# Gated delta rule, gating unit: prompt values turned in 32x32 squares on VectorE instead of on TensorE

## The chip, the cores and the metric

The kernel runs on one core of one Trainium2 chip, in one launch. The metric is the device time of that launch in microseconds (us). The core has a matrix engine (TensorE, PE in the rows; its weight loads PEld), a vector engine (VectorE, DVE), a scalar engine (ScalarE, ACT), GpSimd (POOL), which here mostly issues transfers, and SyncE (SP), which issues the weight loads from HBM. Each engine runs its own instructions in program order and waits for others on semaphores.

## The reference

Two layers of a decoder trunk, for a prompt of 1024 tokens and 8 samples of 4 tokens. Layer 0 has gated delta rule heads (mixer A) and chunked spatial gating groups (mixer B); layer 1 has mLSTM heads; each layer has a squared-ReLU MLP of width 4096. What the change touches is mixer B of layer 0:

```
def spatial_gating(u, v, w_s, b_s):          # chunks of C = 128 tokens, 4 groups of 128 channels
    w = jnp.where(causal_mask(C), w_s[:, :C, :C], 0.0)
    vc = v.reshape(B, NC, C, G_B, DG_B)
    z = jnp.einsum('gpq,bnqgc->bnpgc', w, vc) + b_s[:, :C].T[None, None, :, :, None]
    return u * z.reshape(u.shape).astype(u.dtype)
...
proj = h @ w_in
qkv, gate, beta_pre, a_pre, u_pre, v_pre = split_cols(proj, ...)
u = jax.nn.gelu(u_pre)
vb = rmsnorm(jax.nn.gelu(v_pre).reshape(B, L, G_B, DG_B), sgu_norm_g)
o_b = spatial_gating(u, vb, sgu_w, sgu_b)
```

The product over `q` contracts tokens, so the values `vb` must stand with tokens on the partitions, while the projection leaves them with channels on the partitions. Something must turn each tile of 128 tokens by 4 groups of 128 channels.

## The kernel before

**The dense work.** Every large product of the trunk (`piece`) is done three times over on split operands (high times high, low times high, high times low), and fills TensorE nearly without a gap. It goes in units of 24 steps; each unit needs its own 512 KB of weights, which SyncE loads, ScalarE splits into a high part (`whi`, function `hi`) and VectorE into a low part (`wlo`, function `lo`, line L1788). TensorE may begin a unit only when `wlo` of it is there (`w_split`). `whi` is made of the next unit only when TensorE has begun the present one, and stands in ScalarE's queue behind whatever the program put ahead of it. At the end of a unit ScalarE copies the result out of PSUM.

**The mixer.** Between pieces of dense work stand the steps of the delta rule, in an order that `Plan` writes out once for all engines (`gdn`): for a tile of 128 tokens `act`, `sum`, `dec`, `kk`, `kT`, `vT`, then `b1` to `b4` (the inverse of the triangular matrix, its 16x16 blocks by VectorE in `b1` to `b3`), `la` and `lb` for each level, `vn`, `zw`, `o`, `oT`. Tiles 0 to 3 lie beside the input projection of layer 0, tiles 4 to 7 beside the output projection and the first MLP; a ninth tile (`TILES`) holds the 32 sample tokens and has steps of its own (`gdn_rows`).

**Step `dec` before.** TensorE turns the four groups of values with four transposes (L899) into PSUM (`M4(3)`), and signals `vsT`. ScalarE takes the exponential `E`, waits for `vsT`, squares the four groups out of PSUM, takes the logarithm, then waits for `du` (VectorE's `Dm`, L2129) and takes its exponential `D`, then `dtu` (L2133) and its exponential `DTe`, and last copies the four groups, scaled, into `VB` (`vsr`). These ten or so instructions stand ahead of ScalarE's next unit end and next `whi`. VectorE's step `kk` begins with `A` (L2140), which needs `D`; `A` goes through HBM twice (`base_blocks` on GpSimd: out and in ahead of `b1`, out and in ahead of `b4`), and VectorE's `b4` (L2174) lets TensorE's first `la` go. TensorE's `vT` needs `vsr` (the bank `M4(3)`) and `ke` (L2145, which needs `DTe`).

**The loads.** GpSimd issues a tile's operands in `gdn_x` (L2703): chunks 0 to 11 (query, key, value of mixer A), chunks 20 to 23 (values of the gating unit) with channels on the partitions, each one transfer.

Of the kernel before, what the change touches and what calls it, by code (L numbers as in the profile page):

```python
# [8 lines left out]
ACT = mybir.ActivationFunctionType  # L9

P = 128
D = 1024
# [3 lines left out]
NS = NB * LS  # L16
T = NP + NS
TILES = NP // P
H = 4
# [309 lines left out]
def build(nc, x_prompt, x_sample, state_gdn, state_gdn_conv, state_mlstm_c, state_mlstm_n, state_mlstm_m,  # L329
# [4 lines left out]
    with ctx:  # L334
# [293 lines left out]
        def _(pe):  # L628
# [244 lines left out]
            def gdn(t, step, q):  # L873
# [9 lines left out]
                if step == "sum":  # L883
# [5 lines left out]
                        w("vns", t)  # L889
                    s(mm(M4(0)[:, :, 0:n], ones[:, :], m["SQ"][:, 4:8, :]), "ss")  # L890
                    s(mm(M4(1)[:, :, 0:n], ones[:, :], m["SQ"][:, 0:4, :]), "ss")
                elif step == "dec":
                    if t:
                        w("on", t)
                        w("ofa", t)
                    if g:
                        w("act", t - 3)
                    for h in range(H):
                        last = pe.transpose(M4(3)[0:n, h, :], X[:, 20 + h, :], ident[:, :])  # L899
                    s(last, "vsT")  # L900
                elif step == "kk":
                    w("kn")
                    for h in range(H):
# [4 lines left out]
                        last = mm(M4(1)[0:n, h, 0:n], QH[:, 4 + h, :], QH[:, h, :])  # L908
                    s(last, "kq")
                elif step == "kT":  # L910
                    for h in range(H):
                        last = pe.transpose(M4(2)[0:n, h, :], QH[:, 4 + h, :], ident[:, :])
                    s(last, "kT")
                elif step == "vT":
                    w("vsr")
                    w("ke")
                    w("state")
                    for h in range(H):
                        pe.matmul(M4(3)[:, h, :], X[:, 8 + h, :], ident[:, :], is_transpose=True,
                                  start=True, stop=False)  # L920
                        last = mm(M4(3)[:, h, :], m["KB"][:, h, :], St[:, h, :], start=False, stop=True)
# [46 lines left out]
                        s(last, "x")  # L968
                elif step == "zw":
                    w("inv", inv_at(t, lv - 1, 1))  # L970
                    for h in range(H):
                        last = mm(M4(0)[:, h, 0:n], m["VB"][0:n, h, :], WT[0:n, h, 0:n])
                    s(last, "z")
                elif step == "vn":
                    w("inv", inv_at(t, lv - 1, 1))
                    for h in range(H):
                        last = mm(M4(1)[:, h, :], m["XiT"](h), m["RU"][:, h, :])
                    s(last, "vnew")
                elif step == "o":
                    w("vns")  # L980
                    w("qd")
                    for h in range(H):
                        mm(M4(2)[:, h, :], m["QD"][:, h, :], St[:, h, :], start=True, stop=False)
                        last = mm(M4(2)[:, h, :], m["DT"][:, h, :], m["VN"][:, h, :], start=False, stop=True)
                    s(last, "o")
                    for h in range(H):
                        last = mm(M4(3)[:, h, :], m["KD"][:, h, :], m["VN"][:, h, :])
                    s(last, "ds")
                elif step == "oT":
                    w("on")  # L990
                    w("state", t + 2)
                    for h in range(H):
                        last = pe.transpose(M4(3)[:, h, 0:n], m["ON"][0:n, h, :], ident[0:n, 0:n])
                    s(last, "oT")
# [263 lines left out]
        def _(act):  # L1258
# [257 lines left out]
            def gdn(t, step, q):  # L1516
# [3 lines left out]
                w = lambda name, v=t + 1: act.wait_ge(S("g_" + name), v)  # L1520
                s = lambda ins, name: ins.then_inc(S("g_" + name), 1)
                if step == "act":
                    w("xin", 32 * (t + 1))
                    if t:
                        w("qd", t)
                        w("inv", inv_at(t - 1, LB, 0))
# [12 lines left out]
                elif step == "dec":  # L1539
                    w("bc", 16 * (t + 1))  # L1540
                    s(A_(m["E"], m["KB"], ACT.Exp), "E")
                    w("vsT")
                    for h in range(H):
                        last = A_(m["VB"][0:n, h, :], M4(3)[0:n, h, :], ACT.Square, accum_out=small[0:n, 0, h:h + 1])
                    after(mine(last))
                    vssl = mine(A_(small[0:n, 1, :], small[0:n, 0, :], ACT.Ln, bias=epsc[0:n, :], scale=1.0 / P))
                    w("du")
                    s(A_(m["Dm"], m["Dm"], ACT.Exp, scale=-1.0), "D")
                    after(vssl)
                    vssr = mine(A_(small[0:n, 2, :], small[0:n, 1, :], ACT.Exp, scale=-0.5))  # L1550
                    w("dtu")
                    s(A_(m["DT"], m["DT"], ACT.Exp), "DTe")
                    after(vssr)
                    for h in range(H):
                        last = A_(m["VB"][0:n, h, :], M4(3)[0:n, h, :], ACT.Copy, scale=small[0:n, 2, h:h + 1])
                    s(last, "vsr")
                elif step == "vT" and n == NS:
                    w("vT")
# [208 lines left out]
        def _(dve):  # L1767
# [341 lines left out]
            def gdn(t, step, q):  # L2109
# [15 lines left out]
                elif step == "dec":  # L2125
# [6 lines left out]
                    for h in range(H):  # L2132
                        last = STT(m["DT"][0:n, h], m["KB"][0:n, h], gc[:, h:h + 1], mn[:, :],  # L2133
                                   ALU.subtract, ALU.add)
                    s(last, "dtu")
                elif step == "kk":
                    w("D")
                    w("kk")
# [387 lines left out]
        def _(pool):  # L2526
# [173 lines left out]
            def gdn_x(t, late):  # L2700
# [22 lines left out]
                if t:  # L2723
                    pool.wait_ge(S("g_qn"), t)
                    pool.wait_ge(S("g_vT"), t)
                if t == TILES:
                    pool.wait_ge(S("g_lo"), t)
                load(0, 12, "g_xin")
                load(20, NCH, "g_xin")
                if t not in (0, 4):  # L2730
                    decay_rows(t)
                if t == TILES:
# [231 lines left out]
```

## Time and profile before

| | |
|---|---|
| median of 3 runs | 2590.41 us (2590.01 to 2590.78) |
| profiled execution | 2587.41 us |
| its span in the trace | 2585.0 us |
| mean granted TensorE clock over the span | 0.992 |
| TensorE, VectorE, ScalarE, GpSimd busy | 97%, 53%, 43%, 10% of the span |

The profile is of one execution. The span runs from the first to the last instruction in the trace; 2.4 us of the execution lie around it. The profiled execution is 3.0 us shorter than the median of the runs. In the rows "L630" is the one line through which all matmuls go; which product it is shows in the names (`dense` or `mixer`). L1267 is ScalarE's one line in the same way. `arena` is the mixer's working memory.

### The profile page before, as it was taken

The numbers are of one execution on the slowest core, as the hardware profiler recorded it, in microseconds if no ns is written. First come the engines' busy times: TensorE is split into PE (matmuls) and PEld (weight loads), VectorE is DVE, ScalarE is ACT, GpSimd is POOL, SyncE is SP. The second block draws the span as 40 slices with busy tenths as digits, with TensorE's granted clock in tenths as the row PEclk, the third lists the DMA queues.
The fourth block names the chain that finished last, engine by engine and source line by source line (L and its number), as shares of the span: only waits on it lengthen the run. The fifth ranks groups of instructions, "written<-read, shape, count | busy, mean of one in ns | idle before, by whom it ended". The sixth has DMA issues, their size and how long they took to land.

```text
span 2585.0 us, 40052 instructions
## 1 busy us (share of the span) xinstructions
PE 2519.1 (97%) x16699; PEld 2255.0 (87%) x16699; DVE 1362.7 (53%) x2215; ACT 1114.0 (43%) x1869; POOL 261.1 (10%) x421
## 2 busy tenths in 40 slices
PE   8998989999999999999999999999999999999999
PEld 7778888787787798899999989998887988999998
DVE  4746764655565565434444465535554466443344
ACT  6554446454555344333333345434333345323324
POOL 4121111100001001100001001111111000000000
PEclk9999999999999999999999999999999999999999
DMA  6563335533334366544333235554445343333222
GB/s 206 160 165 109 107 108 138 161 91 96 110 91 118 91 175 186 156 120 114 107 90 106 91 116 171 166 146 134 122 133 157 115 143 98 98 107 115 83 89 84
DMA packets 369396, 321.52 MB, mean 124 GB/s; under 512 B 12601, under 2 KB 340339, under 8 KB 369216
## 3 DMA queue, kind: packets, MB, share of 16 engines
q1 hardware_dynamic: 336224, 207.91, 27.6%
q0 software_dynamic: 32992, 111.06, 14.5%
q8 instruction: 132, 2.16, 0.4%
q14 instruction: 48, 0.39, 0.0%
HBM read 261.33 MB, written 57.58 MB: 123 GB/s over the span
## 4 chain that ended last, share of the span: by engine, by line
PE 85%; DVE 6%; ACT 5%; DMA 2%; issue 2%; POOL 0%; DVEq 0%; ACTq 0%; POOLq 0%
PE dense L630 77%; PE mixer L630 6%; DVE wlo L1788 1%; ACT arena L1267 1%; ACT whi L1267 1%; DVE arena L2022 1%; DVE arena L2024 0%; DVE hf L1929 0%; ACT relu L1267 0%; DMA arena<-xrow 0%; PE mixer L696 0%; ACT L1267 0%; ACT L1272 0%; DVE arena L2258 0%; ACT h1hi L1267 0%
## 5 line engine op out<-in xcount | busy, mean ns | idle before, releaser
L630 PE MATMUL dense<-hhi,whi 128*128 128x272 f32 (+1 forms) x3072 | 847.4, 330 | 22.1 <-DVE wlo L1788 16.9
L630 PE MATMUL dense<-hhi,wlo 128*128 128x272 f32 (+1 forms) x3072 | 826.9, 324 | 0.0
L630 PE MATMUL dense<-hlo,whi 128*128 128x272 f32 (+1 forms) x3072 | 825.7, 323 | 0.0
L1788 DVE TENSOR_TENSOR wlo<-wst,whi 128x1024 fp32r<-128x1024 f32 x384 | 469.4, 1222 | 230.3 <-ACT whi L1267 229.4
L630 PEld LDWEIGHTS dense<-hhi,whi 128*128 128x128 f32 x3072 | 517.2, 189 | 77.3 <-DVE wlo L1788 22.4
L1267 ACT ACTIVATE whi<-wst 128x1024 fp32r<-128x1024 f32 x384 | 403.7, 1051 | 416.5 <-PE dense L630 409.4
L630 PEld LDWEIGHTS dense<-hhi,wlo 128*128 128x128 f32 x3072 | 515.5, 190 | 41.7
L630 PEld LDWEIGHTS dense<-hlo,whi 128*128 128x128 f32 x3072 | 517.8, 190 | 38.2 <-issue 0.7
L630 PE MATMUL dense<-h1hi,whi 128*128 128x272 f32 (+1 forms) x1536 | 422.3, 329 | 11.9 <-DVE wlo L1788 5.8
L630 PE MATMUL dense<-h1hi,wlo 128*128 128x272 f32 (+1 forms) x1536 | 413.5, 323 | 0.0
L630 PE MATMUL dense<-h1lo,whi 128*128 128x272 f32 (+1 forms) x1536 | 411.6, 322 | 0.0
L630 PEld LDWEIGHTS dense<-h1hi,whi 128*128 128x128 f32 x1536 | 256.6, 188 | 41.0 <-DVE wlo L1788 10.0
L1804 DVE TENSOR_TENSOR h1lo<-relu,h1hi 128x544 fp32r<-128x544 f32 (+1 forms) x128 | 90.5, 707 | 358.8 <-ACT relu L1267 358.6
L630 PEld LDWEIGHTS dense<-h1hi,wlo 128*128 128x128 f32 x1536 | 256.8, 188 | 21.4
L630 PEld LDWEIGHTS dense<-h1lo,whi 128*128 128x128 f32 x1536 | 256.6, 188 | 20.7 <-issue 0.5
L1267 ACT ACTIVATE relu<-dense 128x512 f32<-128x512 f32 (+2 forms) x132 | 80.4, 609 | 352.1 <-PE dense L630 352.1
L630 PEld LDWEIGHTS mixer<-arena 128*128 128x128 f32 (+4 forms) x2012 | 142.5, 149 | 42.8 <-issue 20.8
L630 PE MATMUL mixer<-arena 128*128 128x128 f32 (+8 forms) x2012 | 165.6, 257 | 14.4 <-DVE arena L2174 6.4
L1863 DVE TENSOR_TENSOR accA<-dense,accA 128x512 f32<-128x512 f32 (+1 forms) x168 | 116.7, 699 | 91.1 <-PE dense L630 90.5
L1879 DVE TENSOR_TENSOR ssum<-ssum,sq 128x512 f32<-128x512 f32 (+1 forms) x98 | 69.2, 706 | 125.8 <-ACT sq L1267 125.7
L1267 ACT ACTIVATE ffh<-dense 128x512 f32<-128x512 f32 (+5 forms) x124 | 62.2, 525 | 167.0 <-PE dense L630 154.9
L2642 POOL DMA_DIRECT2D proj<-ffh x96 | 52.6, 549 | 462.6 <-ACT ffh L1267 374.6
(398 smaller groups left out, 1792.4 us busy)
## 6 DMA issues: line engine op xcount, KB each, us to landing
wst<-in_w_ff_dram SPq DMA_DIRECT2D x256, 512.0 KB, 3.9
wst<-in_w_in_even_dram SPq DMA_DIRECT2D x48, 512.0 KB, 4.1
wst<-in_w_in_odd_dram SPq DMA_DIRECT2D x48, 512.0 KB, 3.9
proj<-ffh POOLq DMA_DIRECT2D x48, 272.0 KB, 2.6
proj<-ffh POOLq DMA_DIRECT2D x48, 256.0 KB, 2.3
arena<-proj POOLq DMA_DIRECT2D x24, 512.0 KB, 4.9
out_dram<-arena POOLq DMA_DIRECT2D x17, 512.0 KB, 4.7
wst<-in_w_out_even_dram SPq DMA_DIRECT2D x16, 512.0 KB, 4.0
```

Source lines behind the costliest of these rows:

```text
L630: return pe.matmul(out, lhsT, rhs, start=start, stop=stop)
L1267: return act.activation(out, in_, func, **how)
L1788: TT(wlo[:, u % 2, :], wst[:, u % 2, :], whi[:, u % 2, :].bitcast(F32), ALU.subtract)\
L1804: TT(h1lo[:, k, 0:n], r, h1hi[:, k, 0:n].bitcast(F32), ALU.subtract)\
L1863: TT(v, out_of(key, g), v, ALU.add).then_inc(S("dve_evac"), 1)
L1879: ins = TT(ssum[:, 0:n], ssum[:, 0:n], sq2[:, c % 2, 0:n], ALU.add)
L2022: link(TT(tmp, left.unsqueeze(2).broadcast_to([NBLK, b, b, b]), right.rearrange("p j c -> p c j").unsqueeze(1).broadcast_to([NBLK, b, b, b ...
L2642: dma(proj[l][c, :, G0[g]:G0[g] + n], pout2[:, i % 2, 0:n]).then_inc(S(f"stored{i % 2}"), 16)
```

## The change

- **TensorE.** The four transposes of step `dec` go for tiles 0 to 7. Waits that stood there move: `on` to step `kT`, `ofa` to `vT`; `vT` no longer waits for `vsr`, which `zw` now does.
- **GpSimd.** For tiles 0 to 7 the load of chunks 20 to 23 becomes four transfers of 32 partitions each, which put 32x32 squares at the places where they must stand after a full turn. Only the inside of each square is then still unturned.
- **VectorE.** One transpose of 128x512 in 32x32 squares, after `dtu` in step `dec` and ahead of `A` (and of a `wlo`, where the plan has one between them).
- **ScalarE.** `D` now comes before the wait for `vsT`, and `DTe` before the small exponential. Squares and scaled copies read from the working memory instead of PSUM, for prompt tiles.

```
@@ TensorE @@
-                elif step == "dec":
-                    if t:
-                        w("on", t)
-                        w("ofa", t)
-                    if g:
-                        w("act", t - 3)
-                    for h in range(H):
-                        last = pe.transpose(M4(3)[0:n, h, :], X[:, 20 + h, :], ident[:, :])
-                    s(last, "vsT")
@@
                 elif step == "kT":
+                    if t:
+                        w("on", t)
@@
                 elif step == "vT":
-                    w("vsr")
                     w("ke")
                     w("state")
+                    if t:
+                        w("ofa", t)
@@
                 elif step == "zw":
                     w("inv", inv_at(t, lv - 1, 1))
+                    w("vsr")
@@ ScalarE @@
                 if step == "act":
-                    w("xin", 32 * (t + 1))
+                    w("xin", 80 * t + (32 if n == NS else 80))
@@
                 elif step == "dec":
                     w("bc", 16 * (t + 1))
                     s(A_(m["E"], m["KB"], ACT.Exp), "E")
+                    w("du")
+                    s(A_(m["Dm"], m["Dm"], ACT.Exp, scale=-1.0), "D")
                     w("vsT")
-                    for h in range(H):
-                        last = A_(m["VB"][0:n, h, :], M4(3)[0:n, h, :], ACT.Square, accum_out=small[0:n, 0, h:h + 1])
+                    if 0 < t < TILES:
+                        w("ds", t)
+                    values = m["VB"] if n == P else M4(3)[0:n]
+                    for h in range(H):
+                        last = A_(m["KD" if n == P else "VB"][0:n, h, :], values[:, h, :], ACT.Square,
+                                  accum_out=small[0:n, 0, h:h + 1])
                     after(mine(last))
                     vssl = mine(A_(small[0:n, 1, :], small[0:n, 0, :], ACT.Ln, bias=epsc[0:n, :], scale=1.0 / P))
-                    w("du")
-                    s(A_(m["Dm"], m["Dm"], ACT.Exp, scale=-1.0), "D")
+                    w("dtu")
+                    s(A_(m["DT"], m["DT"], ACT.Exp), "DTe")
                     after(vssl)
                     vssr = mine(A_(small[0:n, 2, :], small[0:n, 1, :], ACT.Exp, scale=-0.5))
-                    w("dtu")
-                    s(A_(m["DT"], m["DT"], ACT.Exp), "DTe")
                     after(vssr)
                     for h in range(H):
-                        last = A_(m["VB"][0:n, h, :], M4(3)[0:n, h, :], ACT.Copy, scale=small[0:n, 2, h:h + 1])
+                        last = A_(m["VB"][0:n, h, :], values[:, h, :], ACT.Copy, scale=small[0:n, 2, h:h + 1])
                     s(last, "vsr")
@@ VectorE, end of step dec @@
+                    if g:
+                        w("act", t - 3)
+                    else:
+                        w("xin", 80 * (t + 1))
+                    if t:
+                        w("oT", t)
+                    s(dve.transpose(rows_of(m["VB"]), rows_of(X[:, 20:NCH])), "vsT")
@@ GpSimd, gdn_x @@
+                    pool.wait_ge(S("g_vsT"), t)
...
                 load(0, 12, "g_xin")
-                load(20, NCH, "g_xin")
+                if t == TILES:
+                    load(20, NCH, "g_xin")
+                else:
+                    squares = X[:, 20:NCH].rearrange("p c (b i) -> p (c b) i", i=32)
+                    for a in range(4):
+                        c0 = t * P + 32 * a
+                        dma(squares[32 * a:32 * a + 32],
+                            proj[0][20:NCH, :, c0:c0 + 32].rearrange("c (b j) i -> j (c b) i", j=32))\
+                            .then_inc(S("g_xin"), 16)
```

**ScalarE in tile 4**, from the exponential `E` (which waits for `g_bc`) to the next `whi`. Here `arena<-mixer` is a read out of PSUM, and `accA<-dense` and `sq<-accA` belong to the output projection. Before:

```order
L1267 ACTIVATE arena<-arena 128x512 [waits g_bc]
L1267 ACTIVATE arena,small<-mixer 128x128 [waits g_vsT]
L1267 ACTIVATE arena,small<-mixer 128x128 x3
L1267 ACTIVATE small<-small,epsc 128x4 [waits act_step]
L1267 ACTIVATE arena<-arena 128x512 [waits g_du]
L1267 ACTIVATE small<-small 128x4 [waits act_step]
L1267 ACTIVATE arena<-arena 128x512 [waits g_dtu]
L1267 ACTIVATE arena<-mixer,small 128x128 [waits act_step]
L1267 ACTIVATE arena<-mixer,small 128x128 x3
L1267 ACTIVATE accA<-dense 128x512 [waits job_done]
L1267 ACTIVATE sq<-accA 128x512 [waits act_evac,squares_added]
L1267 ACTIVATE whi<-wst 128x1024 [waits w_loaded1,w_used]
```

And now:

```order
L1262 ACTIVATE arena<-arena 128x512 [waits g_bc]
L1262 ACTIVATE arena<-arena 128x512 [waits g_du]
L1262 ACTIVATE arena,small<-arena 128x128 [waits g_ds,g_vsT]
L1262 ACTIVATE arena,small<-arena 128x128 x3
L1262 ACTIVATE small<-small,epsc 128x4 [waits act_step]
L1262 ACTIVATE arena<-arena 128x512 [waits g_dtu]
L1262 ACTIVATE small<-small 128x4 [waits act_step]
L1262 ACTIVATE arena<-arena,small 128x128 [waits act_step]
L1262 ACTIVATE arena<-arena,small 128x128 x3
L1262 ACTIVATE accA<-dense 128x512 [waits job_done]
L1262 ACTIVATE sq<-accA 128x512 [waits act_evac,squares_added]
L1262 ACTIVATE whi<-wst 128x1024 [waits w_loaded1,w_used]
```

The exponential that waits for `g_du` has moved ahead of the squares, which wait for `g_vsT`, now VectorE's signal.

**VectorE in tile 2**, from `Dm` to `ke` (`ffh` is the convolution beside it). Before:

```order
L2129 SCALAR_TENSOR_TENSOR arena<-arena,cols,maskpos 128x128 [waits g_bc,dve_step]
L2129 SCALAR_TENSOR_TENSOR arena<-arena,cols,maskpos 128x128 x3
L2133 SCALAR_TENSOR_TENSOR arena<-arena,cols,masknegT 128x128 x4
L1788 TENSOR_TENSOR wlo<-wst,whi 128x1024 [waits w_hi]
L1827 SCALAR_TENSOR_TENSOR ffh<-ffh,par 128x512 [waits act_evac]
L1830 SCALAR_TENSOR_TENSOR ffh<-ffh,par 128x32
L2140 SCALAR_TENSOR_TENSOR arena<-mixer,cols,arena 128x128 [waits g_kk,g_D,dve_step]
```

And now:

```order
L2128 SCALAR_TENSOR_TENSOR arena<-arena,cols,maskpos 128x128 [waits g_bc,dve_step]
L2128 SCALAR_TENSOR_TENSOR arena<-arena,cols,maskpos 128x128 x3
L2132 SCALAR_TENSOR_TENSOR arena<-arena,cols,masknegT 128x128 x4
L2141 STREAM_TRANSPOSE arena<-arena 128x512 [waits g_oT,g_xin]
L1787 TENSOR_TENSOR wlo<-wst,whi 128x1024 [waits w_hi]
L1826 SCALAR_TENSOR_TENSOR ffh<-ffh,par 128x512 [waits act_evac]
L1829 SCALAR_TENSOR_TENSOR ffh<-ffh,par 128x32
L2146 SCALAR_TENSOR_TENSOR arena<-mixer,cols,arena 128x128 [waits g_kk,g_D,dve_step]
```

One instruction is inserted, ahead of a `wlo` and of `A`; the others keep their order.

## Rows read from the trace of the kernel before

The line numbers are those of the kernel before.

**Rows 1.** Page, part 1: busy us (share of the span) xinstructions.
```profile
PE 2519.1 (97%) x16699; PEld 2255.0 (87%) x16699; DVE 1362.7 (53%) x2215; ACT 1114.0 (43%) x1869; POOL 261.1 (10%) x421
```

**Rows 2.** Timeline, TensorE, tile 5: start us, us, engine, line, operation [idle before].
```profile
568.17 0.60 PE L899 MATMUL mixer<-ident,arena 128*128 128x128 f32 x4
568.52 0.48 PE L630 MATMUL dense<-h1hi,whi 128*128 128x512 f32 x1
568.84 0.39 PE L630 MATMUL dense<-h1lo,whi 128*128 128x512 f32 x1
569.06 0.40 PE L630 MATMUL dense<-h1hi,wlo 128*128 128x512 f32 x1
```

**Rows 3.** Line L2185, VectorE: duration ns min/median/max.
```profile
L2185 DVE STREAM_TRANSPOSE arena<-arena x8: 310/311/313, 178.1 to 785.4; 128x128 f32<-128x128 f32 x8
```

**Rows 4.** Timeline, VectorE and GpSimd, mLSTM tile 0.
```profile
1167.53 1.42 DVE L2362 STREAM_TRANSPOSE arena<-arena 128x256 f32<-128x256 f32 x4
...
1170.47 3.13 POOL L2839 DMA_DIRECT2D arena<-proj  x4
```

**Rows 5.** Timeline, ScalarE, VectorE and TensorE, tile 4.
```profile
425.18 0.25 ACT L1267 ACTIVATE arena<-mixer 128x128 f32<-128x128 f32 x1
...
426.33 0.30 ACT L1267 ACTIVATE small<-small,epsc 128x4 f32<-128x4 f32 x1
...
428.14 0.63 ACT L1267 ACTIVATE arena<-arena 128x512 f32<-128x512 f32 x1 [0.33 <-DVE arena L2133]
...
428.68 1.12 ACT L1267 ACTIVATE arena<-mixer,small 128x128 f32<-128x128 f32 x4
...
429.68 0.61 ACT L1267 ACTIVATE accA<-dense 128x512 f32<-128x512 f32 x1
...
426.98 1.13 DVE L2133 SCALAR_TENSOR_TENSOR arena<-arena,cols,masknegT 128x128 f32<-128x128 f32 x4
...
434.49 1.21 DVE L1788 TENSOR_TENSOR wlo<-wst,whi 128x1024 fp32r<-128x1024 f32 x1
...
435.76 0.52 PE L630 MATMUL dense<-hhi,whi 128*128 128x272 f32 x2 [1.00 <-DVE wlo L1788]
```

**Rows 6.** Timeline, VectorE and TensorE, tile 6.
```profile
663.16 1.23 DVE L1788 TENSOR_TENSOR wlo<-wst,whi 128x1024 fp32r<-128x1024 f32 x1 [0.25 <-ACT whi L1267]
...
665.42 0.40 PE L630 MATMUL dense<-h1hi,whi 128*128 128x512 f32 x1
```

**Rows 7.** Timeline, VectorE and TensorE, tile 7.
```profile
748.39 1.23 DVE L1788 TENSOR_TENSOR wlo<-wst,whi 128x1024 fp32r<-128x1024 f32 x1 [2.67 <-ACT whi L1267]
...
750.95 0.39 PE L630 MATMUL dense<-hhi,whi 128*128 128x512 f32 x1
```

**Rows 8.** Timeline, VectorE and TensorE, tiles 1 to 3.
```profile
210.81 1.12 DVE L2140 SCALAR_TENSOR_TENSOR arena<-mixer,cols,arena 128x128 f32<-128x128 f32 x4
...
237.05 0.62 PE L630 MATMUL mixer<-arena 32*32 32x16 f32 x32 [5.38 <-DVE arena L2174]
...
345.79 0.82 PE L630 MATMUL dense<-hhi,whi 128*128 128x272 f32 x2 [6.34 <-DVE wlo L1788]
```

**Rows 9.** TensorE's timeline, then windows: us, busy of PE, PEld, DVE, ACT, POOL, PEclk, DMA share, GB/s.
```profile
600.30 0.71 PE L630 MATMUL dense<-hhi,whi 128*128 128x512 f32 x1 [1.93 <-DVE wlo L1788]
...
600.00:604.00 4.00, 3.70 (x9) 2.94 (x10) 2.17 (x3) 1.45 (x2) 0.92 (x1) 0.57 0.63 164
```

**Rows 10.** Timeline, ScalarE, VectorE and TensorE, sample tile.
```profile
830.15 0.25 ACT L1267 ACTIVATE arena<-mixer 32x128 f32<-32x128 f32 x1
...
830.96 0.35 DVE L2063 SCALAR_TENSOR_TENSOR arena<-arena,gcol,maskposS 128x128 f32<-128x128 f32 x1
...
835.65 0.50 PE L630 MATMUL dense<-h1hi,whi 128*128 128x512 f32 x1 [0.51 <-DVE h1lo L1804]
```

**Rows 11.** Timeline, TensorE, tile 0.
```profile
155.44 0.30 PE L919 MATMUL mixer<-ident,arena 128*128 128x128 f32 x1 [1.06 <-ACT arena L1267]
...
170.31 0.50 PE L630 MATMUL dense<-hhi,whi 128*128 128x512 f32 x1 [1.40 <-DVE wlo L1788]
```

## The prediction

> **What bounds the kernel now.** I read the page first. TensorE is busy 97% of the span and no other engine is near [rows 1], so the end is set by TensorE's instructions plus its waits. Each change has to be read as one or the other. Next I went through the timeline of TensorE around each of the eight tiles, looking for gaps and for who ended them. Last I read ScalarE and VectorE just ahead of those gaps. What a reader is to see there: most of TensorE's waits near the mixer end with a `wlo` or with `b4`, both VectorE's, and behind `wlo` stands a `whi` of ScalarE. So the question is not only what TensorE saves but what ScalarE and VectorE now do later.
>
> **What TensorE saves.** In tile 5 the four transposes begin at 568.17 and the next dense product at 568.52, which is 0.35 us; that product is followed after 0.32 us, where the next pair stands 0.22 us apart [rows 2]. So a group costs about 0.35 + 0.09 = 0.44 us, and eight groups 3.5 us. The mean duration of such a transpose is no help, since they overlap. The saving counts only where TensorE does not wait for somebody else soon after.
>
> **What VectorE pays.** The trace has no 128x512 transpose in squares. A 128x128 one took 0.311 us [rows 3]; four of 128x256 took 1.42 us together, 0.355 us each [rows 4]. From above the price is two of the latter, 0.71 us, from below one of them, 0.36 us. Between them I go by pace: a `wlo` of 1024 columns took 1.21 us [rows 5], so half as many columns are worth 0.61 us, which I take.
>
> **What GpSimd pays.** The mLSTM loads its values in the same way; issuing four such transfers took 3.13 us [rows 4]. They replace one issue, so GpSimd is at most 3.1 us later per tile. Behind them stand the row of decays for the next tile and the stores of the projection; the values themselves are wanted half a tile later. I cost this at nothing. The cover is that distance of tens of us; without it 3.1 us a tile would show.
>
> **What ScalarE pays.** This is the step that I think decides. Before, the squares began when TensorE's transposes were done (425.18 in tile 4), while VectorE was still at `Dm`. ScalarE then had only `D`, the small exponential, `DTe` and the copies left: VectorE's `dtu` ended at 426.98 + 1.13 = 428.11, `DTe` began at 428.14, the copies at 428.68, and ScalarE was free at 429.68 [rows 5]. Now the squares wait for VectorE's transpose, which ends at about 428.11 + 0.6 = 428.7. Behind it come the squares, 426.33 - 425.18 = 1.15 us, the logarithm, 0.30, `DTe`, 428.68 - 428.14 = 0.54, and the small exponential, some 0.1 [rows 5]. The copies begin at 430.8 instead of 428.68: **ScalarE is 2.1 us later** wherever VectorE was the one waited for. The squares and copies now read from SBUF. The nearest rows are an exponential of 128x512 from SBUF, 0.63 us, and a copy of 128x512 from PSUM, 0.61 us [rows 5], so 0.02 us each or 0.2 us over eight, which I leave out of the sum; it is inside the range.
>
> The Trainium skill ("VectorE: DVE Perf Modes", section "The TRN2 errata — SBUF-src ops pay a fixed extra latency per instruction") gives ScalarE 224 fixed cycles from SBUF and 172 from PSUM at 1.2 GHz. That is an estimate of 0.35 us for the eight instructions, which in tiles 4, 6 and 7 would add 1.0 us to the sum below. The rows above show less of it, and the sum goes by them.
>
> **Tile by tile.**
> *Tile 0:* nothing. TensorE waited 1.06 us for `vsr`, and this wait goes. But it also waits at 170.31 for a `wlo` [rows 11]; ahead of that `wlo` ScalarE and VectorE work on without a gap on instructions whose total is unchanged, and TensorE's start there stays where it was.
> *Tiles 1 to 3:* `A` follows `dtu` directly in tile 1, at 210.81, and from there the way through HBM and `b1` to `b3` leads to TensorE's wait of 5.38 us at 237.05; in tile 3 a `wlo` behind `b3` ends a wait of 6.34 us [rows 8]. Tile 2 is built alike. Here VectorE's chain sets the time, not TensorE: its 0.61 us more delay each tile by 0.6 us, TensorE's saving is swallowed, and so is ScalarE's 2.1 us, which is less than the waits. Together **+1.8 us**.
> *Tile 4:* TensorE waits 1.00 us for the `wlo` that begins at 434.49 [rows 5]. VectorE gets there by way of a sum of squares for which ScalarE's copies must be done, then `A`, `ke` and two more without a gap. The 2.1 us go straight through: TensorE starts at 437.9 instead of 435.76, **+2.1 us**, and its wait grows to some 3.5 us.
> *The clock:* after a wait of 1.93 us the granted clock was 0.57 over the next four us, with products at 0.63 us where they take 0.40 [rows 9, 2]; this is mostly the lower of TensorE's two levels, 1.2 instead of 2.4 GHz. The loss is 0.43 x 3.70 = 1.6 us. I expect it behind tile 4's long wait. Part of it falls on TensorE while it would wait for the norm's chain, so I take **+1.4 us**.
> *Tile 5:* no unit begins there while ScalarE is late: **-0.4 us**.
> *Tile 6:* from the start of a `wlo` to TensorE's first product were 435.76 - 434.49 = 1.27 us [rows 5]. `wlo` at 663.16 allowed 664.43, TensorE needed it at 665.42: a slack of 1.0 us [rows 6]. Late by 2.1, it costs **+1.1 us**.
> *Tile 7:* 748.39 + 1.27 = 749.66 against 750.95, a slack of 1.3 us [rows 7]: **+0.8 us**.
> *Sample tile:* its squares began at 830.15, ahead of `Dm`; now they follow `D`, which needs VectorE's `Dm`, done at 830.96 + 0.35 = 831.31. That is some 1.3 us later for the copies and all behind them, and TensorE already waits for an `h1lo` at 835.65 [rows 10]: **+1.3 us**.
>
> The sum is 0 + 1.8 + 2.1 + 1.4 - 0.4 + 1.1 + 0.8 + 1.3 = 8.1 us. On the profiled execution's 2587.4 us this gives 2595.5 us. The median of the runs shown was 3.0 us above that execution, so I forecast 2590.4 + 8.1 = 2598.5, rounded to **2598 us**. The likeliest case's own range is 2594 to 2602: the transpose between 0.36 and 0.71 us moves seven tiles by -0.25 to +0.1 us each, and the clock's loss may be none.
>
> **The rivals.**
> *Faster.* ScalarE's lateness never reaches a `wlo` that TensorE wants, because ScalarE catches up in its idle time, and VectorE's `D` comes sooner. For it speaks that ScalarE is idle more than half the span [rows 1] and that tile 0 loses a wait of 1.06 us [rows 11]. Then TensorE keeps its 3.5 us, perhaps the 1.06 too: 2586 to 2587 us. Against it stands the slack of only 1.0 and 1.3 us in tiles 6 and 7. It decides if ScalarE is late by less than 1.0 us. Chance 0.12.
> *Half covered, no clear change.* Tiles 6, 7 and the sample tile hide it, and the clock stays up: 1.8 + 2.1 - 3 x 0.4 = +2.7, so 2593 us. Chance 0.25.
> *The clock falls more often.* Each new wait, in tiles 2, 6 and 7, brings the low level. Three times 1.6 us on top: 2603 us. For it speaks the wait of 1.93 us, after which the first product took 0.71 us [rows 9]; against it that of 1.00 us, after which the first took 0.52 [rows 5]. Chance 0.08.
> *The squares in HBM.* The transfers in pieces of 32 numbers hold up a weight load or a store. Were each tile late by the 3.13 us of issuing alone [rows 4], the eight would cost 25 us, 2615. The mLSTM does it without TensorE waiting for it, so 0.05. The Trainium skill ("DMA: Bandwidth & Descriptors", section "Why small descriptors are slow (HBM only)") speaks for this case: each descriptor carries fixed costs that weigh most below 256 bytes. No row here shows what that does to this load.
> The forecast has the remaining 0.50.
>
> **How the numbers follow.** A measurement of this kernel can tell about 0.2% from no change, 5.2 us. Slower than 2595.6 are most of the forecast (0.43 of 0.50), the clock and the transfers: 0.57 with a little of the second rival. Within the bound lie the rest of the forecast and nearly all of the second rival: 0.31. Faster is 0.12. The range runs from 2588, which takes in the second rival and the edge of the first, to 2603.
>
> **What the profile of the changed kernel would show.** Right: in tile 4, ScalarE's copies at about 2.1 us further behind `Dm` than before and a wait of TensorE for `wlo` of 3 us or more, with the granted clock below 1 behind it; new waits for `wlo` of 1 us or so in tiles 6 and 7; the waits for `b4` in tiles 1 to 3 still there; the transpose at 0.6 to 0.7 us. Wrong: TensorE without new waits from tile 4 on, `DTe` or the copies at their old distance from `Dm`, or the squares' transfers landing so late that ScalarE's `act` waits for them.

## The result, and the profile after

Before 2590.21 us (median of 6 runs, 2585.59 to 2590.94), after 2600.32 us (6 runs, 2595.82 to 2603.27). The ratio is 1.0044, 95% interval [1.0034, 1.0054]: slower by 10 us by the medians and by some 11 by the ratio. A second set of five runs of the same changed kernel gave 2599.53 us against 2587.51 us, 1.0052 [1.0038, 1.0066].

The profiled execution of after took 2603.27 us, the slowest of its six, with a span of 2601.5 us. Page, part 1, to lay beside [rows 1]:

```profile
PE 2522.2 (97%) x16667; PEld 2255.6 (87%) x16667; DVE 1368.3 (53%) x2223; ACT 1117.0 (43%) x1869; POOL 275.7 (11%) x445
```

TensorE has 32 instructions fewer and its busy time is no shorter; VectorE has gained 5.6 us, ScalarE 3.0, GpSimd 14.6. The busy shares explain nothing. The waits of TensorE do (us in total, times, longest us):

```profile
PE dense L630 <- DVE wlo L1787: 27.4, 18, 4.7
PE mixer L630 <- DVE arena L2180: 7.0, 2, 5.1
PE mixer L913 <- DVE arena L2151: 5.9, 4, 2.1
...
PE dense L630 <- DVE h1lo L1803: 3.6, 4, 1.9
```

Before, `wlo` had stood at 22.6 us in 15 waits, `b4` (now L2180) at 6.4, `h1lo` (the low part of the MLP's activations) at 1.9. The third line is new: TensorE's `vT` (L913) waits for VectorE's `ke` (L2151).

To place the loss I took the start of the same TensorE instruction in both traces and followed the difference. It was 0.2 us at 140, 3.8 behind tile 0, 4.3 behind tile 3 (425), 8.6 behind tile 4 (481), 8.1 at 568, 12.2 behind the sample tile (836), 16.7 at 1985. A single trace of before is a poor zero, though, and so is one of after. That is what the second pair of profiles below is for.

**Tile 4**, the timeline of after for ScalarE, VectorE and TensorE, then a window behind the wait (us, busy of PE, PEld, DVE, ACT, POOL, PEclk, DMA share, GB/s):

```profile
433.51 0.31 ACT L1262 ACTIVATE arena<-arena 128x128 f32<-128x128 f32 x1 [1.04 <-DVE arena L2141]
...
434.83 0.30 ACT L1262 ACTIVATE small<-small,epsc 128x4 f32<-128x4 f32 x1
435.03 0.62 ACT L1262 ACTIVATE arena<-arena 128x512 f32<-128x512 f32 x1
...
435.77 1.28 ACT L1262 ACTIVATE arena<-arena,small 128x128 f32<-128x128 f32 x4
436.96 0.57 ACT L1262 ACTIVATE accA<-dense 128x512 f32<-128x512 f32 x1
...
432.77 0.70 DVE L2141 STREAM_TRANSPOSE arena<-arena 128x512 f32<-128x512 f32 x1
438.29 0.69 DVE L1878 TENSOR_TENSOR ssum<-ssum,sq 128x512 f32<-128x512 f32 x1 [4.81 <-ACT sq L1262]
438.90 1.12 DVE L2146 SCALAR_TENSOR_TENSOR arena<-mixer,cols,arena 128x128 f32<-128x128 f32 x4
...
441.73 1.22 DVE L1787 TENSOR_TENSOR wlo<-wst,whi 128x1024 fp32r<-128x1024 f32 x1
...
443.00 0.52 PE L630 MATMUL dense<-hhi,whi 128*128 128x272 f32 x2 [3.99 <-DVE wlo L1787]
...
444.00:448.00 4.00, 4.00 (x17) 2.96 (x16) 1.23 (x1) 2.84 (x4) 2.72 (x6) 0.57 0.93 286
```

This is the chain of the prediction. `Dm` began at 425.93 before and begins at 430.67 here. From there the copies stand at +5.10 us instead of +2.75, so ScalarE is 2.35 us later. `wlo` stands at +11.06 instead of 434.49 - 425.93 = +8.56, later by 2.50. TensorE's wait is 3.99 us instead of 1.00, and the granted clock behind it is 0.57, most of the time at the lower level, where the kernel before had 1.00. The squares go from 433.51 to the logarithm at 434.83, 1.32 us where [rows 5] had 1.15; the copies free ScalarE after 1.19 us instead of 1.00.

**Tiles 6 and 7 and the sample tile**, TensorE's timeline of after; in [rows 6, 7] the first two had no wait, in [rows 10] the third had 0.51:

```profile
673.46 0.50 PE L630 MATMUL dense<-h1hi,whi 128*128 128x512 f32 x1 [1.82 <-DVE wlo L1787]
...
761.66 0.51 PE L630 MATMUL dense<-hhi,whi 128*128 128x512 f32 x1 [1.51 <-DVE wlo L1787]
...
847.84 0.50 PE L630 MATMUL dense<-h1hi,whi 128*128 128x512 f32 x1 [1.85 <-DVE h1lo L1803]
```

**Tiles 1 to 3**, which I had not foreseen in this form. VectorE in tile 3, then TensorE in tiles 1 to 3, then the window behind the first of these waits:

```profile
330.83 0.70 DVE L2141 STREAM_TRANSPOSE arena<-arena 128x512 f32<-128x512 f32 x1
331.45 1.08 DVE L2146 SCALAR_TENSOR_TENSOR arena<-mixer,cols,arena 128x128 f32<-128x128 f32 x4
333.73 0.69 DVE L2151 SCALAR_TENSOR_TENSOR arena<-arena 128x512 f32<-128x512 f32 x1 [1.19 <-ACT arena L1262]
...
218.28 0.33 PE L913 MATMUL mixer<-ident,arena 128*128 128x128 f32 x1 [1.96 <-DVE arena L2151]
...
276.82 0.41 PE L913 MATMUL mixer<-ident,arena 128*128 128x128 f32 x1 [2.11 <-DVE arena L2151]
...
334.48 0.33 PE L913 MATMUL mixer<-ident,arena 128*128 128x128 f32 x1 [1.17 <-DVE arena L2151]
...
219.00:223.00 4.00, 4.00 (x23) 4.00 (x21) 2.25 (x8) 2.90 (x9) 2.55 (x4) 0.59 0.20 29
```

The diff put `DTe` behind the squares. So in tiles 1 and 3 VectorE, done with `A`, waits 1.19 us for `DTe` ahead of `ke`, and TensorE's `vT` waits for `ke`, though it lost its wait for `vsr`. In tile 2 it is not `DTe`: a `wlo` and the convolution stand between the transpose and `A` there, `ke` follows `A` without a gap, and TensorE waits 2.11 us all the same.

**The parts' prices.** VectorE's transpose (duration ns min/median/max, first and last start us), and the loads in squares on GpSimd with their time to landing:

```profile
L2141 DVE STREAM_TRANSPOSE arena<-arena x8: 702/703/708, 151.4 to 755.1; 128x512 f32<-128x512 f32 x8
...
L2742 POOL DMA_DIRECT2D arena<-proj x32: 649/653/675, 132.5 to 680.5; - x32
...
DMA to landing us min/median/max: 4.7/6.1/7.2
```

### The profile page after: what moved, and what is told of

Read it like the earlier page. It is cut to its first block, busy times and chain, and to the rows that moved or that the text cites. A ratio compares the mean times of both kernels' runs of the same rounds, so it can differ in the third digit from the quotient of the medians.

```text
span 2601.5 us, 40036 instructions
## 1 busy us (share of the span) xinstructions
PE 2522.2 (97%) x16667; PEld 2255.6 (87%) x16667; DVE 1368.3 (53%) x2223; ACT 1117.0 (43%) x1869; POOL 275.7 (11%) x445
## 4 chain that ended last, share of the span: by engine, by line
PE 77%; DVE 5%; ACT 4%; issue 2%; DMA 1%; POOL 0%; DVEq 0%; ACTq 0%; POOLq 0%
PE dense L630 71%; PE mixer L630 5%; DVE wlo L1787 1%; ACT arena L1262 1%; ACT whi L1262 1%; ACT relu L1262 0%; DVE hf L1928 0%; ACT h1hi L1262 0%; DVE arena L2264 0%; DVE hlo L1924 0%; PE mixer L1181 0%; DVE accA L1862 0%; DVE arena L2021 0%; DMA arena<-in_state_mlstm_c_dram 0%; DMA out_dram<-arena 0%
```

## The experiments

The twelve experiments came in three groups of four. The kernel before ran beside each group, with medians of 2586.28, 2587.51 and 2587.14 us, and each ratio below is to the kernel before of its own group. The expectations of the first group were written in us from the 2590 of the first measurement, so compare the ratios. Theory A: ScalarE's lateness, by way of `wlo` and `ke`, is the loss. Its rival B: the loads in squares and GpSimd's longer work are.

**DTe ahead of the squares.**

```diff
 s(A_(m["Dm"], ..., ACT.Exp, scale=-1.0), "D")
+w("dtu")
+s(A_(m["DT"], m["DT"], ACT.Exp), "DTe")
 w("vsT")
...
-w("dtu")
-s(A_(m["DT"], m["DT"], ACT.Exp), "DTe")
```

> The change, with one step of ScalarE moved: the exponential of DT (DTe) stands ahead of the four squares instead of behind them. Theory A (order on ScalarE): in the changed kernel VectorE waits 1.19 us ahead of ke for DTe in each prompt tile, and TensorE's vT then waits 1.2 to 2.1 us for ke in tiles 1 to 3. Both waits go; the copies stay as late as they were, so the waits for wlo in tiles 4, 6 and 7 stay in part. Time 3 to 6 us below the changed kernel's 2600.3, so 2594 to 2597. Theory B (the loads in pieces and the longer work of GpSimd cost the time, from tile 0 on): no clear difference from the changed kernel, 2599 to 2601.

Measured: 2599.43 us, 1.0051 [1.0038, 1.0064]. No gain. VectorE's gap ahead of `ke` went (`ke` follows `A` after 1.00 us in tiles 1 and 3) and the waits at `vT` fell from 5.9 us in 4 to 2.8 in 2; that of tile 2 stayed at 2.10. What TensorE did not wait for at `vT` it waited for later: in tile 1 the wait at `vT` went from 1.96 to 0.67 us and that for `b4` from 5.14 to 6.83, in tile 3 the 1.17 us went and a wait for `wlo` grew from 0.66 to 1.56. The copies came at +4.72 us behind `Dm`, 0.4 earlier, and tile 4 still cost 4.8 us. So the wait at `vT`, the most striking new line of the profile, was not where the time went.

**The transpose early, ScalarE's old order.**

```diff
 elif step == "dec":
+    ... s(dve.transpose(rows_of(m["VB"]), rows_of(X[:, 20:NCH])), "vsT")
     w("bc", 16 * (t + 1))
     (Dm, DT)
-    ... s(dve.transpose(...), "vsT")
 ScalarE: E, squares, logarithm, D, small exponential, DTe, copies, as in the kernel before
```

> The change, with VectorE's transpose put ahead of Dm (and of its wait for bc) and ScalarE's steps in the order of the kernel before (E, squares, logarithm, D, small exponential, DTe, copies); the sample tile's order is thereby also the old one. Theory A: ScalarE is as early as before, D some 0.7 us later; vT's waits go, wlo in tiles 4, 6 and 7 is at its old place, h1lo in the sample tile waits 0.5 us again. TensorE keeps a part of its 3.5 us: 2587 to 2591. Theory B: tile 0 still costs 3.8 us and the whole stays at 2597 to 2600. A third (VectorE's 0.7 us in front of A is what costs): 2 to 4 us above the kernel before, 2592 to 2594.

Measured: 2594.52 us, 1.0027 [1.0018, 1.0037]. It lies between the expectations of A and B, and 7 us above its kernel before where the third had 2 to 4: about half of the loss came back. The copies are at +2.76 us behind `Dm` again in tiles 1 to 7. In its trace TensorE lost 1.0 us in tile 4 and nothing in tiles 6, 7 and in the sample tile's step at `h1lo`. Most of what stayed arose earlier: TensorE was 6.2 us behind the kernel before at 425. So in tiles 0 to 3 the loss did not go with ScalarE's lateness.

**One plain load.**

```diff
-squares = ...; for a in range(4): dma(squares[32 * a:32 * a + 32], ...)
+load(20, NCH, "g_xin")
```

> The change, but the values come with the one plain load of the kernel before instead of four loads of turned squares, so that the squares are turned within themselves but not in place: the delta rule's values are permuted, all instructions of the engines stay. It prices the loads and GpSimd's issues alone. Theory B: tile 0's 3.8 us go and the time falls by 4 to 10 us, to 2590 to 2596. Theory A: at most 1 us of the 3.8 goes, 2599 to 2601.

Measured: 2599.23 us, 1.0049 [1.0036, 1.0061]. Its trace had TensorE at -0.65 us behind tile 3 where after had +4.3, but the time is that of the changed kernel: against B as the main cause. (The second trace of after, below, stood at +0.4 there with the loads in squares, so the 4.3 was scatter in the main.)

**ScalarE's new order in the kernel before.**

```diff
+w("du"); s(A_(m["Dm"], ..., scale=-1.0), "D")
 w("vsT")
 (squares, logarithm)
-w("du"); s(A_(m["Dm"], ..., scale=-1.0), "D")
-(small exponential)
 w("dtu"); s(A_(m["DT"], m["DT"], ACT.Exp), "DTe")
+(small exponential)
```

> The kernel before (TensorE transposes, one load, no transpose on VectorE), with only ScalarE's steps in the order of the changed kernel: E, D, squares, logarithm, DTe, small exponential, copies. Theory A: the squares now begin behind D, some 1.5 us later than before, DTe behind them; half or more of the loss shows: 2594 to 2598, with waits of VectorE ahead of ke and of TensorE at vT. If instead VectorE's transpose or the loads cost the time: 2590 to 2592.

Measured: 2589.08 us, 1.0013 [1.0004, 1.0022], a quarter of the loss and less than A expected. ScalarE is late by 1.06 us here (copies at +3.81), not by 2.35. Tile 4's wait is twice what it was, and the sample tile's is that of the changed kernel; TensorE's timeline:

```profile
434.05 0.52 PE L630 MATMUL dense<-hhi,whi 128*128 128x272 f32 x2 [2.08 <-DVE wlo L1788]
...
835.37 0.50 PE L630 MATMUL dense<-h1hi,whi 128*128 128x512 f32 x1 [1.87 <-DVE h1lo L1804]
```

TensorE's difference grew by 0.8 us over tile 4 and by 1.35 in the sample tile. So ScalarE's order alone gives the sample tile's cost. In tile 4 the order alone makes less than half of the lateness (1.06 of 2.35 us); the rest is the transpose behind `dtu`, for which the squares wait, and 0.17 us by which the four squares are slower from SBUF.

**The two kernels again.**

> The changed kernel once more, unaltered, for a second profile and five more times beside the others. If the costs read in its first profile belong to the change, TensorE's offset against the kernel before is again some 3.8 us behind tile 0, 4.3 more from tile 4, 1.6 in tile 6, 1.8 in tile 7, 1.3 in the sample tile. What comes out otherwise is scatter from one execution to the next. The first profiled execution was the slowest of six, so the span should be 2 to 5 us shorter here; ratio to before 1.0035 to 1.0055.

> The kernel before once more, unaltered: it shows how far two profiles of one kernel differ. Expected: the same starts of TensorE within 1 us up to 1970 us; and at 1981 us, where the first profile had no fall of the clock behind the wait for the mLSTM's state and all others had one that cost 1.6 to 2 us, a coin's toss. Ratio 0.999 to 1.001.

Measured: after 2599.53 us, 1.0052 [1.0038, 1.0066]; before 2587.95 us, 1.0004 [0.9996, 1.0013]. TensorE's difference against the first trace of before, for both traces of after and the second of before, in us:

| stretch of before | after | after again | before again |
|---|---|---|---|
| tile 0, 140 to 188 | +3.6 | +2.1 | +0.1 |
| tiles 1 to 3, to 425 | +0.4 | -2.0 | -1.2 |
| tile 4, to 481 | +4.3 | +4.3 | -0.3 |
| tile 5's group, to 568 | -0.5 | -0.4 | 0 |
| 568 to 604 | -1.6 | -1.6 | -1.6 |
| tile 6, to 665.5 | +1.6 | +1.6 | 0 |
| 665.5 to 725 | +1.4 | -1.4 | +1.4 |
| tile 7, 725 to 751.5 | +1.3 | +1.3 | 0 |
| 751.5 to 830 | 0 | +1.3 | 0 |
| step at `h1lo`, 830 to 840 | +1.3 | +2.0 | 0 |
| 840 to 1975 | +2.2 | +1.2 | +0.5 |
| 1975 to 1985 | +2.3 | +3.6 | +0.3 |

What repeats to 0.1 us belongs to the change: tiles 4, 6 and 7. Tiles 1 to 3 scatter by more than 2 us. The row 568 to 604 is the fall of the clock in the first trace of before, which the second does not have though the wait ahead of it is the same. The row 665.5 to 725 is of the same kind: every trace has a wait of 2.68 us at the place where before has it (709.8), and the clock behind it differed from one execution to the next. Behind 840 comes nothing that the diff touches; the 4.1 and 5.1 us that the two traces of after lose from there to the end, where before again has 0.6, no experiment explains. TensorE's timeline and a window, of before again:

```profile
599.11 0.50 PE L630 MATMUL dense<-hhi,whi 128*128 128x512 f32 x1 [1.93 <-DVE wlo L1788]
...
598.00:602.00 4.00, 2.89 (x12) 2.36 (x13) 2.97 (x3) 2.23 (x3) 1.17 (x2) 1.00 0.52 156
```

**The loads in squares in the kernel before.**

```diff
-load(20, NCH, "g_xin")
+for a in range(4): dma(squares[32 * a:32 * a + 32], ...)   # tiles 0 to 7
```

> The kernel before, with only the load changed: the values come in four loads of turned squares, TensorE transposes them as before, so the delta rule's values are permuted. It prices GpSimd's issues and the transfers alone. Theory B (the loads cost some 1.2 us in each of tiles 0 to 2, as the offsets 4.3 against -0.65 of the changed kernel with and without them suggest): 3 to 5 us, 2589 to 2592 where before is 2586.3. Theory A (ScalarE's order and no more; the medians of the two, 1.0044 and 1.0049, say so): 0 to 1 us.

Measured: 2589.47 us, 1.0010 [1.0001, 1.0018], some 2.6 us, at the edge of what can be told. Its trace is of the slowest of its eleven runs; it lost 4.5 us in tile 0 and 0.6 from tile 4 on. Tile 0, TensorE at `b4`, first in the kernel before, which had the clock at 1.00 there, then here with the windows behind:

```profile
175.38 0.44 PE L630 MATMUL mixer<-arena 32*32 32x16 f32 x32 [0.70 <-DVE arena L2174]
...
178.46 0.44 PE L630 MATMUL mixer<-arena 32*32 32x16 f32 x32 [2.14 <-DVE arena L2174]
...
178.00:181.00 3.00, 2.54 (x38) 1.72 (x38) 0.69 (x3) 0.00 (x0) 0.00 (x0) 0.75 0.71 182
181.00:184.00 3.00, 3.00 (x41) 2.41 (x41) 1.48 (x4) 2.07 (x3) 0.56 (x1) 0.68 0.22 86
```

A first part of tile 0's loss stands further ahead, at ScalarE's `whi` near 142. It waits for a load of weights that SyncE issued near 132.3, beside the tile's own loads. ScalarE in the kernel before and here:

```profile
140.76 1.05 ACT L1267 ACTIVATE whi<-wst 128x1024 fp32r<-128x1024 f32 x1
...
142.12 1.06 ACT L1267 ACTIVATE whi<-wst 128x1024 fp32r<-128x1024 f32 x1 [1.20 <-DMA wst<-in_w_in_even_dram]
```

That load landed 9.8 to 10.0 us after its issue in five of the six traces with the loads in squares in tile 0, and 9.0 in the other (the first of after). In the eight with the plain load it took 8.0 to 8.3 us in five and 8.9 to 9.1 in three. ScalarE's wait was 1.2 to 1.4 us in the five, none to 0.5 in all others.

**D first in tiles 1 to 3 of the kernel before.**

```diff
+if t in (1, 2, 3): w("du"); s(A_(m["Dm"], ...), "D")
 w("vsT")
 (squares, logarithm)
-w("du"); s(A_(m["Dm"], ...), "D")
+if t not in (1, 2, 3): w("du"); s(A_(m["Dm"], ...), "D")
```

> The kernel before, with only D (the exponential of Dm) put ahead of the squares on ScalarE in tiles 1 to 3. A new theory C: ScalarE comes 1 us later to whi, frees the staging buffer of the weights later, and SP's next load of 512 KB then starts behind the small transfer of the diagonal blocks (arow) instead of ahead of it; that transfer landed 2.3 to 2.5 us after its issue in all kernels with D first and 3.8 to 4.3 us in those with the squares first. By C tiles 1 to 3 gain 2 to 4 us and nothing is lost behind them: 2582 to 2584. By the simpler view that a later ScalarE only costs: 2586 to 2588.

Measured: 2587.15 us, 0.9997 [0.9989, 1.0006]: no difference. In its trace VectorE's `b1` did come 1.7 us sooner behind `Dm` in tile 1, and TensorE at 425 stood at -1.4 us; but before again stood at -0.9 there with nothing changed. (`b1` waits for the diagonal blocks of `A` to come back from HBM.) Theory C is not shown by the times.

**The change in halves.** The whole change in some tiles only, the others as before.

```diff
+BY_DVE = (0, 1, 2, 3)      # second kernel: (4, 5, 6, 7)
 PE, ACT, DVE, POOL: the new path if t in BY_DVE, else the old one
```

> The change in tiles 0 to 3 alone (loads in squares, VectorE's transpose behind dtu, ScalarE's new order); tiles 4 to 7 and the sample tile are those of the kernel before. Theory A' (ScalarE's lateness costs where TensorE stands close behind it, which is from tile 4 on): the two profiles of the changed kernel had TensorE 0.4 and 4.3 us late behind tile 3, so 0 to 4 us: 2588 to 2592. Theory B' (a part of the loss that the profiles do not show cleanly sits in tiles 0 to 3): 2593 or more.

> The change in tiles 4 to 7 alone; tiles 0 to 3 and the sample tile are those of the kernel before. Theory A': both profiles of the changed kernel lost 4.3 us in tile 4, 1.6 in tile 6 and 1.8 in tile 7 and won 0.45 in tile 5: 7.3 us, so 2593 to 2596. Theory B': less than half of the loss, 2589 to 2591.

Measured: tiles 0 to 3 alone 2591.28 us, 1.0017 [1.0008, 1.0027]; tiles 4 to 7 alone 2593.36 us, 1.0023 [1.0012, 1.0034]. Together 1.0040, and with the sample tile's 1.3 us 1.0045: within their intervals of 0.1% each, the parts add up to the change's 1.0044 and 1.0052. In the second kernel tiles 4, 5, 6 and 7 cost +4.3, -0.5, +1.6 and +1.3 us, as in the table; TensorE in tiles 4 and 6:

```profile
438.64 0.59 PE L635 MATMUL dense<-hhi,whi 128*128 128x272 f32 x2 [3.99 <-DVE wlo L1814]
...
669.05 0.50 PE L635 MATMUL dense<-h1hi,whi 128*128 128x512 f32 x1 [1.82 <-DVE wlo L1814]
```

The first kernel's trace, of the slowest of its ten runs (2596.1 us), lost 4.5 us in tile 0 and 0.9 in tiles 1 to 3. GpSimd's read of `xrow`, the second round trip of the diagonal blocks through HBM, was issued at 174.39, and VectorE's `b4` began when it landed:

```profile
178.34 0.48 DVE L2208 TENSOR_SCALAR arena<-arena,halves 128x128 f32<-128x128 f32 x2 [3.01 <-DMA arena<-xrow]
...
178.88 0.44 PE L635 MATMUL mixer<-arena 32*32 32x16 f32 x32 [2.08 <-DVE arena L2208]
```

**The transpose early, in tiles 4 to 7 only.** The second experiment's place and order, once by itself and once with D first in tiles 1 to 3.

```diff
+BY_DVE = (4, 5, 6, 7)      # transpose ahead of Dm, squares ahead of D
+D_FIRST = ()               # last kernel: (1, 2, 3)
```

> VectorE turns the values in tiles 4 to 7 alone, with the transpose ahead of Dm and ScalarE's old order (as in the second experiment); all else is the kernel before. The profile of the second experiment had +1.0 us in tile 4, -0.45 in tile 5, -0.1 in tile 6 and 0 in tile 7. Theory A': no clear difference, 2586 to 2589. If VectorE's transpose or the load in squares costs something by itself in a stage where TensorE is the bound: 2590 or more.

> As the one with the early transpose in tiles 4 to 7, and D ahead of the squares on ScalarE in tiles 1 to 3 besides. It is the version that the parts found so far would make the fastest. By the sum of the parts (0.5 and -0.8 us): 2585 to 2588, not clearly below the kernel before; by theory C in full (2 to 4 us won in tiles 1 to 3): 2583 to 2585.

Measured: 2585.93 us, 0.9998 [0.9989, 1.0007], and 2586.22 us, 0.9994 [0.9985, 1.0003]. Moved ahead, VectorE's transpose costs nothing in tiles 4 to 7, and the waits in tiles 6 and 7 are gone. Against the experiment with the whole change in tiles 4 to 7, the loads in squares, the transposes and the missing work of TensorE are the same; only the places on VectorE and ScalarE differ, and the loss of 1.0023 is gone. But it gains nothing either. In tile 4 it stands in front of `Dm` and passes its 0.65 us on, TensorE's wait there being 2.26 us:

```profile
435.24 0.52 PE L635 MATMUL dense<-hhi,whi 128*128 128x272 f32 x2 [2.26 <-DVE wlo L1814]
```

That is +1.0 us in tile 4 against -0.5, -0.1 and -0.4 in the other three. (In the last kernel's trace tile 4 cost 2.4 us, since the clock fell behind the same wait.) The same place and order in all tiles had 1.0027, so the early transpose with its loads costs some 0.3%, 7 us, in tiles 0 to 3, and the late one, at 1.0017, not more (each ratio is good to 0.1%). No version was clearly faster than the kernel before.

## Why the prediction was right, and where its steps were off

The forecast of 2598 us in 2588 to 2603 met 2600.32, and the mechanism given the most weight holds: ScalarE's lateness, by way of `wlo`, from tile 4 on. Undoing it in tiles 4 to 7 takes 1.0023 to 0.9998. That the number came so close is in part luck. The loss forecast was 8.1 us; measured it was 10 by the medians, and 12 in the second set, where the kernel before stood at 2587.51 and not at the 2590.4 of the forecast. Two places stood at nothing in the sum and cost 2 to 4 us (tile 0) and 4 to 5 us (behind 840) in the traces, against less than the 1.8 us forecast in tiles 1 to 3; what else makes the sum fall only 2 to 4 us short is scatter of that size between executions. Step by step:

- *TensorE saves 0.44 us a tile.* In tile 5, the one that hides nothing, every trace with the transposes gone gained 0.44 to 0.48 us. Right.
- *VectorE pays 0.61 us.* The transpose took 0.70 us, and VectorE's next instruction began 0.63 us after its start. So 0.63 is what `A` is later by, and 0.70 what the squares wait for. The upper bound was misread: the 1.42 us of [rows 4] are four instructions that overlap, one of 128x256 took 0.40 us (median of 32), not 0.355.
- *ScalarE is 2.1 us later; reading from SBUF is left out.* The copies came 2.35 us later and ScalarE was free 2.5 us later. The some 0.4 us missing are VectorE's transpose, 0.09, and the reading from SBUF, 0.36: 1.32 against 1.15 us for the squares, 1.19 against 1.00 for the copies. This is the term that was mis-sized: 0.02 us an instruction where it measured 0.045. I had read it from exponentials and copies that ran in one piece of 512 columns, and took their durations; what counts is the distance from start to start in a row of four. The Trainium skill's rule ("VectorE: DVE Perf Modes", section "The TRN2 errata — SBUF-src ops pay a fixed extra latency per instruction"), by which the estimate was 0.35 us for the eight, agrees with the measured 0.36.
- *Tile 4, 2.1 and the clock 1.4.* Measured 4.3 in three traces, and 4.9 in that with one plain load, where the clock behind the wait was 0.50. The start of the `wlo` product was 3.0 us later than its surroundings, the clock behind it (0.57) took the rest, 1.3 us. The mechanism right, ScalarE's term too small.
- *Tile 5, -0.4.* -0.4 to -0.5.
- *Tile 6, 1.1, and tile 7, 0.8.* 1.6 and 1.3: with 2.5 us of lateness instead of 2.1, less the slacks of 1.0 and 1.3, it is 1.5 and 1.2.
- *Sample tile, 1.3.* 1.3 and 2.0 in the two traces, the second with a fall of the clock behind it, 1.35 with ScalarE's order alone.
- *Tile 0: nothing. GpSimd and the transfers: nothing.* This step failed. Tile 0 took 3.6 and 2.1 us. In the first trace the read of `xrow` was issued 1.7 us later than before and took 3.65 us to land instead of 2.97, TensorE waited 1.89 us for `b4`, and the low clock stood behind it (windows of after):

```profile
175.00:178.00 3.00, 1.11 (x31) 0.63 (x33) 0.48 (x2) 0.00 (x0) 0.03 (x1) 0.99 0.88 187
178.00:181.00 3.00, 3.00 (x31) 1.99 (x19) 0.28 (x1) 0.00 (x0) 0.00 (x0) 0.50 0.32 98
```

  In the second trace the read took 2.94 us and TensorE waited 0.89 us, little more than before; there ScalarE's wait of 1.43 us for the weights at 142 was the greater part. I had asked when the values are wanted and not what else is in flight beside them: SyncE's load of weights, and the round trip of the diagonal blocks, which GpSimd issues too. In the six traces with the loads in squares in tile 0 the stretch from 140 to 188 took 2.1 to 4.5 us more than in the first trace of before; in the seven others it took 0.1 to 1.4 more.
- *Tiles 1 to 3, 1.8, from VectorE's transpose ahead of `A`.* Not confirmed as such: +0.4, -2.0 and +0.9 us in three traces, with a scatter as large. I missed that `DTe` behind the squares holds up `ke` and `vT` in tiles 1 and 3; that wait is real, and moving it away bought nothing. Tiles 0 to 3 together cost 1.0017, some 4 us, twice the 1.8 forecast, and tile 0 is the greater part in the trace.

Of the rivals, "the clock falls more often" came in small part: it fell in tile 2 of the first trace, not of the second, and in no trace behind the waits of tiles 6 and 7. The rival on the transfers had the mechanism, a weight load held up, but in tile 0 alone; with their loads alone changed the cost was some 2.6 us where the rival had 25. What stays open: the price of the loads in squares. Alone they cost 1.0010 [1.0001, 1.0018] in the kernel before, but taking them out of the changed kernel did not make it faster. And tiles 0 to 3's 4 us are not split further between loads, order and transpose; with the transpose early and the old order they were not less. Nor is the wait for the mLSTM's state near 1981 settled: it was 2.8 us in both traces of after, with the clock at 0.66 and 0.50 behind it, and 2.0 and 2.3 in those of before with the clock up; kernels that differ only in other places had either.

## What to carry to other kernels

When work moves from TensorE to another engine, ask what becomes ready later on a third one. Here, from tile 4 on, the 0.7 us of VectorE mattered little by themselves; the transpose was placed behind `dtu`, ScalarE's squares waited for it, and from there 2.5 us went through to every product that TensorE stood close behind. Then look at the slack at each such product: a lateness less than the slack is free, the rest is paid in full.

A new wait in the list of waits is not yet a loss. The waits at `vT` in tiles 1 and 3 were removed, and later ones grew by about as much.

Profile both kernels twice before explaining 1 or 2 us of a single trace.

## What the runs showed of the hardware

- A wait of TensorE does not settle its clock. After the same wait of 1.93 us in tile 5 the granted clock was 0.57 in one trace of before [rows 9] and 1.00 in the other. In all fourteen traces TensorE waited 2.68 us where before has it at 709.8; in the six us behind it the clock was 0.75 in the first trace of before, 0.50 in the second and 1.00 in the second of after. Here are the wait in before and the three windows, in this order:

```profile
709.83 0.60 PE L630 MATMUL mixer<-arena 32*32 32x32 f32 x15 [2.68 <-issue]
...
710.00:716.00 6.00, 6.00 (x35) 4.62 (x33) 2.48 (x4) 4.25 (x4) 0.00 (x0) 0.75 0.50 151
...
707.00:713.00 6.00, 5.93 (x29) 4.74 (x30) 2.48 (x4) 4.29 (x5) 0.00 (x0) 0.50 0.42 136
...
714.00:720.00 6.00, 5.88 (x45) 4.54 (x46) 2.79 (x7) 4.61 (x6) 0.00 (x0) 1.00 0.54 167
```

  After tile 4's waits of 3.6 to 4.0 us the clock fell in all five traces that had them, to 0.50 to 0.58 in the four us that begin within 1.1 us of the wait's end. After those of 2.1 to 2.3 us it was 1.00 in three and 0.65 in one.
- A transfer of 32 KB (the read of `arow`, the first round trip of the diagonal blocks) in tile 1 landed 4.2 us after its issue in the kernel before and 2.5 with ScalarE's new order in it. In the former SP's next load of weights (512 KB) was issued at 214.89, ahead of it at 215.36; in the latter at 217.15, behind it at 216.61, since `wlo`, which frees the staging buffer, ended at 217.13 instead of 214.87. It is an observation; the times did not show a gain from it.
- VectorE's transpose in squares of 32 took 0.70 us for 128x512 (the changed kernel, 8 instances), 0.40 for 128x256 (32 instances) and 0.31 for 128x128 [rows 3].
- The ScalarE squares and copies of 128x128 that moved from PSUM to SBUF took 0.045 us more each, from start to start in a row of four.
